# Eight gate blocks of a hybrid mixer as four 2x2 quadrant products with seven products each, weight sums on GpSimd

## What is computed

```
proj = h @ w_in                      # h: 512 x 1024
(r_q, r_k, r_v, r_g, m_q, m_k, m_v, m_o, m_i, m_f, gate_r, gate_m) = split(proj)
ret = head_rms_norm(retention_chunkwise(rq, rk, rv))
ret = ret * ret_gn_w * silu(r_g)
y_ret = ret @ w_ret_branch
hm = mlstm_chunkwise(mq, mk, mv, i_pre, f_pre) * sigmoid(m_o)
hm = head_rms_norm(hm) * mlstm_gn_w
y_m = hm @ w_mlstm_branch
merged = sigmoid(gate_r) * y_ret + sigmoid(gate_m) * y_m
x = x + merged @ w_out
```

## Time and profile before

| | us |
|---|---|
| median of 3 runs | 1042.69 |
| lowest and highest | 1042.02, 1044.81 |
| profiled execution, first to last instruction | 1040.3 |
| mixer, start of the gate blocks to their end | 219.6 to 420.4 |
| last matmul of the experts starts | 1030.57 |

### The profile page before, as it was taken

One profiled execution on the slowest core, in us unless ns is written; L12 is line 12 of the kernel. 1 busy time (PEld: TensorE's weight loads), 2 busy tenths in 40 slices (PEclk: granted clock), 3 DMA queues, 4 the chain that ended last, 5 costly groups with the idle time before them and its releaser, 6 DMA issues.

```text
span 1040.3 us, 12422 instructions
## 1 busy us (share of the span) xinstructions
PE 1016.0 (98%) x4701; PEld 649.2 (62%) x4701; DVE 428.2 (41%) x744; ACT 276.7 (27%) x472; POOL 71.4 (7%) x101
## 2 busy tenths in 40 slices
PE   8999999999999999999999999999999999999896
PEld 7888888888888888888886433333333333333333
DVE  5265356434533324544625223333333333333235
ACT  6343555333333334622313110000000000000012
POOL 0683000000000000000000100000000000000000
PEclk9999999999999999999999999999999999999999
DMA  9224222222222223224789799999999999999993
GB/s 326 81 82 151 64 72 80 81 81 81 82 81 82 81 81 115 89 87 163 292 323 405 302 421 420 421 420 420 421 420 420 420 420 421 420 421 421 420 415 147
DMA packets 60400, 263.97 MB, mean 254 GB/s; under 512 B 9328, under 2 KB 9520, under 8 KB 35640
## 3 DMA queue, kind: packets, MB, share of 16 engines
q1 hardware_dynamic: 57464, 257.32, 62.6%
q0 software_dynamic: 2624, 5.78, 1.5%
q10 hardware_dynamic: 256, 0.10, 0.0%
HBM read 263.17 MB, written 4.20 MB: 257 GB/s over the span
## 4 chain that ended last, share of the span: by engine, by line
PE 74%; SPq 18%; DMA 3%; DVE 2%; issue 1%; ACT 1%; DVEq 0%
PE pj L492 46%; SPq L393 13%; PE pj L712 11%; PE pj L738 6%; SPq L390 5%; DMA raw_moe<-in_w_up_dram 3%; PE cb L449 3%; PE cb L748 2%; PE cb L749 1%; DMA raw_mix<-in_w_in_dram 1%; PE cb L512 1%; PE cb L541 1%; DVE sg L1555 1%; PE cb L545 1%; PE cb L548 0%
## 5 line engine op out<-in xcount | busy, mean ns | idle before, releaser
L712 PE MATMUL pj<-raw_moe,xT 128*64 128x512 f32 x1016 | 227.6, 595 | 4.4 <-DMA raw_moe<-in_w_up_dram 2.6
L1184 DVE TENSOR_TENSOR wl<-raw_mix,wh 128x1024 fp32r<-128x1024 f32 x88 | 110.5, 1257 | 186.5 <-ACT wh L893 186.4
L712 PEld LDWEIGHTS pj<-raw_moe,xT 128*64 128x64 f32 x1016 | 72.1, 137 | 141.0 <-issue 141.0
L492 PE MATMUL pj<-wh,hTh 128*128 128x512 f32 x320 | 127.3, 398 | 0.8 <-DVE hTl L1215 0.8
L893 ACT ACTIVATE wh<-raw_mix 128x1024 fp32r<-128x1024 f32 x88 | 93.0, 1059 | 129.8 <-PE pj L492 124.0
L492 PE MATMUL pj<-wl,hTh 128*128 128x512 f32 x320 | 124.9, 390 | 0.0
L492 PE MATMUL pj<-wh,hTl 128*128 128x512 f32 x320 | 124.6, 389 | 0.0
L738 PE MATMUL pj<-raw_moe,hf 128*64 128x512 f32 x512 | 116.7, 598 | 1.6 <-ACT hf L1129 1.6
L1537 DVE TENSOR_TENSOR x<-x,cb 128x512 f32<-128x512 f32 x120 | 76.9, 683 | 98.9 <-PE cb L749 98.9
L492 PE MATMUL pj<-hTh,wh 128*128 128x512 f32 x192 | 76.8, 400 | 0.0
L738 PEld LDWEIGHTS pj<-raw_moe,hf 128*64 128x64 f32 x512 | 34.6, 136 | 67.1 <-issue 67.0
(11 more groups left out here) (296 smaller groups left out, 1235.6 us busy)
## 6 DMA issues: line engine op xcount, KB each, us to landing
raw_moe<-in_w_gate_dram SPq DMA_DIRECT2D x64, 1024.0 KB, 26.8
raw_moe<-in_w_down_dram SPq DMA_DIRECT2D x64, 1024.0 KB, 26.7
raw_moe<-in_w_up_dram SPq DMA_DIRECT2D x63, 1024.0 KB, 26.1
raw_mix<-in_w_in_dram SPq DMA_DIRECT2D x32, 1024.0 KB, 5.1
raw_mix<-in_w_ret_branch_dram SPq DMA_DIRECT2D x4, 1024.0 KB, 5.0
raw_mix<-in_w_mlstm_branch_dram SPq DMA_DIRECT2D x4, 1024.0 KB, 5.9
raw_mix<-in_w_out_dram SPq DMA_DIRECT2D x4, 1024.0 KB, 5.0
xt<-in_x_dram SPq DMA_DIRECT2D x4, 512.0 KB, 6.6
```

The lines of the kernel that those rows point to most:

```text
L492: m = nc.tensor.matmul(pj[:, i, :], lhsT, rhs, start=k == 0 and n == 0, stop=k == KD - 1 and n == 2)
L712: mm = nc.tensor.matmul(pj[a * CAP:(a + 1) * CAP, up, :], xT[:, 4 * half + k, a * CAP:(a + 1) * CAP], weights_of(m + a)[:, k, :], start=ha ...
L1184: V.tensor_tensor(wl[:, q % RING, :, :], raw_mix[n % MIX_RAW][:, 2 * (q % 2):2 * (q % 2) + 2, :], wh[:, q % RING, :, :].bitcast(F32), ALU. ...
```

## The change

The two blocks of each gate are taken together as one product of 512 x 1024 by 1024 x 1024, and both factors are cut into quadrants: h into tokens 0 to 255 and 256 to 511 by inputs 0 to 511 and 512 to 1023, the weights into inputs by columns 0 to 511 and 512 to 1023. In Strassen's scheme (Winograd's form) seven products of quadrants and of their sums give all four result quadrants. Such a product is 256 tokens x 512 inputs x 512 columns, in two halves s (`product_half`). The seven are named by their weights: `U_11`, `U_21`, `U_T1`, `U_22`, `U_T2`, `U_T3`, `U_T4`; four of them take a sum of weight quadrants, four a sum of parts of h (`second`, `first21`, `fourth` and a third, which replaces a part of h).

- A product accumulates on the bank of an earlier one; ACT or DVE copies or adds the bank into an SBUF home between the two (`fast_evict`, `upper_left`, `upper_right`, `lower_right`). Sigmoids are then taken from the home (`gate_sigmoid`).
- Each pair has 14 ring entries (two per product) in place of 8.
- GpSimd forms the sums of h (`combined`: ten operations of 128x1024), the 32 sums of weights (`weight_sum`), in place in `raw_mix`, which gets a fourth place, and the gating of the retention (`ret_gated`). ACT scales the retention by its norm first (`ret_scaled`).
- In the channel-major pairs a matmul streams 256 tokens, so there are twice as many at half the width.
- The 16 mLSTM steps are spread over the 28 halves of the first two pairs by `ATTENTION`, which comes out as after halves 1, 3, 4, 6, 8, 10, 11, 13, 15, 17, 18, 20, 22, 24, 25, 27. The first four turns stand in the last pair, the others in blocks 16 and 17 (`TURNS`).

The core of the diff:

```diff
+FAST = (B_RG, B_GR, B_GM, B_MO)
+U_11, U_21, U_T1, U_22, U_T2, U_T3, U_T4 = range(7)
+ATTENTION = [1 + (26 * i + 7) // 15 for i in range(16)]
...
+            def product_half(p, u, s):
...
+                ah, al = parts[u]
+                columns = FAST[p] in (B_GR, B_GM)
+                for v in range(2):
+                    q = fast_entry(p, u, v)
+                    if s == 0:
+                        pe.wait_ge(wl_ok, q + 1)
+                    for kk in range(2):
+                        k = 2 * v + kk
+                        for c in range(2 if columns else 1):
...
+                            for n, (lhsT, rhs) in enumerate(ops):
+                                m = nc.tensor.matmul(o, lhsT, rhs, start=u in (U_11, U_21, U_T1) and k == 0 and c == 0 and n == 0,
...
+            for p in range(len(FAST)):
+                for u in range(PRODUCTS):
+                    for s in range(2):
+                        x = 2 * (PRODUCTS * p + u) + s
+                        product_half(p, u, s)
+                        if x == 0:
+                            ml_scores(0)
+                        if x in ATTENTION:
+                            i = ATTENTION.index(x)
+                            ml_products(*divmod(i, 4))
+                            if i < 15:
+                                ml_scores(i + 1)
...
+            def fast_half(p, u, s):
...
+                if pu == U_21:
+                    upper_left(pp, ps)
+                if pu == U_T3:
+                    lower_right(pp, ps)
...
+                if after >= 0:
+                    ml_state(after)
+                if x == 1:
+                    dve.wait_ge(dt_ok, H)
+                    ml_weighted(0)
+                if 0 <= after < 15:
+                    ml_weighted(after + 1)
+                mix_tail(fast_entry(p, u, s) + LEAD)
+                if pu == U_T2:
+                    upper_right(pp, ps)
+                if x in (1, 3, 7):
+                    part_tail((1, 3, 7).index(x) + 1)
...
+            def weight_sum(p, n, v):
+
+                if n == 0:
+                    pool.wait_ge(wl_ok, fast_entry(p, U_11, v) + 1)
+                    pool.wait_ge(*fast_landed(p, U_T3))
...
+                dst, term = ((U_11, U_T3), (U_11, U_22), (U_T3, U_22), (U_11, U_21))[n]
+                ks = slice(2 * v, 2 * v + 2)
+                t = raw_mix[role(p, dst)][:, ks, :]
+                G.tensor_tensor(t, t, raw_mix[role(p, term)][:, ks, :], ALU.add).then_inc(sum_ok, 1)
...
+            pool.wait_ge(r_s, 16)
+            combined(fourthf, secondf, ((hTh[:, high, lower], ALU.add), (hTl[:, high, lower], ALU.add)))
+            weight_sums(0, 0)
+            pool.wait_ge(mqk_ok, 8)
+            combined(thirdf, hTh[:, low, lower].bitcast(F32),
+                     ((hTh[:, low, upper], ALU.subtract), (hTl[:, low, lower], ALU.add), (hTl[:, low, upper], ALU.subtract)))
+            weight_sums(0, 1)
+            weight_sums(0, 2)
```

More of the change, by code:

```diff
@@ new lines, in _ @@
+            turned = {2 * (PRODUCTS * w[0] + w[1]) + w[2]: n[0] for w, n in TURNS.items() if len(w) == 3}
+            for b in range(B_RG):
+                evict_block(b - 1)
+                block_of(b)
+            evict_block(B_RG - 1)
+            ret_output(15)
+            root(2, 16)
+            for p in range(len(FAST)):
+                for u in range(PRODUCTS):
+                    for s in range(2):
+                        fast_half(p, u, s)
+            fast_evict(*half_before(FAST_HALVES))
@@ L1357, in _, with ml_normed, block_of @@
                     merged_tail(ct)
-                if b == BLOCKS:
-                    break
+            def ml_normed(half, n):
+                dve.wait_ge(sq_ok, TT * (n + 2))
+                rstd(3 + n, ssq[:, 8 * half:8 * half + 8], 8, DV)
+                for t in range(TT):
+                    for a in range(2):
+                        hv = mva[:, t, 2 * half + a, 0:DV]
+                        m = V.tensor_scalar(hv, hv, stat[:, 2, 4 * a + t:4 * a + t + 1], None, ALU.mult)
+                m.then_inc(hm_ok, 1)
+            def block_of(b):
                 if b == B_WM + 1:
@@ L1460, in _ @@
+            for s in range(2):
+                ml_gated(1, 0, s)
+            for b in range(B_WR, BLOCKS):
+                evict_block(b - 1)
+                block_of(b)
+            evict_block(BLOCKS - 1)
             for t in range(TT):
@@ L1689, in _, with combined @@
             pool.dma_start(gbc[:, :, :], g_dram.to_broadcast([P, H, T])).then_inc(gb_in, 16)
+            G = nc.gpsimd
+            lower, upper = slice(0, 256), slice(256, 512)
+            low, high = slice(0, 4), slice(4, KD)
+            def combined(dst, first, terms):
+                for n, (term, op) in enumerate(terms):
+                    m = G.tensor_tensor(dst[:, :, :], (dst if n else first)[:, :, :], term.bitcast(F32), op)
+                    if n < len(terms) - 1:
+                        own(m)
+                m.then_inc(rope_ok, 1)
@@ L1691, in _ @@
+            for s in range(2):
+                weight_sum(1, 0, s)
+                ret_gated(1, 0, s)
+            for p in range(1, len(FAST)):
+                for n in range(1 if p == 1 else 0, 4):
+                    weight_sums(p, n)
             pool.wait_ge(st_in, 16 * TT)
```

596 lines of the change are left out of this document (430 added, 166 removed).

## The result

| | before | after |
|---|---|---|
| median of the runs, us | 1042.7 (5 runs) | 1046.5 (5 runs, 1045.3 to 1050.2) |
| ratio, 95% interval | | 1.0042, 1.0024 to 1.0060 |
| profiled execution, span, us | 1040.3 | 1043.5 |
| first matmul on the merged rows (block `B_WO`), us | 511.2 | 514.1 |

The change makes the kernel 0.4% slower: 96 matmuls of 0.2269 us are gone and nothing of it arrives. The prediction had 1041.7 and gave the faster side the larger chance, so it is wrong in direction, though its range holds the time.

What follows compares the result with a forecast made beforehand. The prediction took TensorE (PE) to bound the kernel. Its terms, -21.8 + 2.3 + 8.5 + 1.5 + 3 + 3 + 2.5 = -1.0 us, took the span from 1040.3 to 1039.3, so a median of 1041.7 us; range 1028 to 1056.

Steps and rivals of the forecast that it cites:

- matmuls removed: Eight gate blocks: array time of 672 matmuls in place of 768, 96 fewer at 0.2269 us; 21.8 us less.
- narrow matmuls: Two channel-major pairs: 672 matmuls of 256 columns in place of 336 wide ones; 2.3 us more.
- stall at the seam: Start of the first pair, 219.6 us: norm steps wait for GpSimd operations, masked scores come late; PE idle 8.5 us.
- half rate after stalls: Behind the seam's stall: PE drops to 1.2 GHz, some 3 us at half rate; 1.5 us more.
- next attention step: Step one half after that of half 3: VectorE tails behind GpSimd sums delay its scores; 3 us, bounds 0 and 4.5.
- pairs of steps later on: Attention steps after halves 10-11, 17-18 and 24-25: 1 us of stall each, 3 us.
- steady pairs: Pairs without attention: turns of GpSimd sums and VectorE tails fill 96% of 38.1 us; 2.5 us for the two pairs.
- Rival A: Gate stretch: the turns are hidden and the products pay; about 1030 us, chance 0.28.
- Rival B: Gate stretch: shared turns become the bound, some 4 us more in each of the last three pairs; about 1054, chance 0.22.
- Rival C: Channel-major pairs: narrow matmuls are bound by weight loads, from 0.135 us per matmul; 1055 to 1090 us, chance 0.06.

Runs made afterwards that it cites:

- run 5: The changed kernel with GpSimd's third sum over h made to wait for the 16 roots of retention's norm; 1043.2 us, ratio 1.0004.
- run 1: The changed kernel with GpSimd's 32 sums of weights cut to 4 of their 512 columns; 1033.8 us, ratio 0.9908.
- run 3: The changed kernel with unread filler matmuls, 20 before the first attention products and 9 before the ninth; 1045.0 us, ratio 1.0023.
- Run 4: The changed kernel with 512-column matmuls in the channel-major pairs; 1535.7 us with other gate numbers, first matmul on merged rows at 511.0 against 514.1.
- Run 6: The changed kernel with ScalarE's squares of two mLSTM rows moved behind the last gate sigmoid; 1044.1 us, ratio 1.0012.
- kernel 8: The changed kernel with third h sum behind the norm, last sigmoid before the squares, weight sums on VectorE, norm writing its roots directly; 1032.3 us, ratio 0.9893.
- kernel 10: kernel 8 with the sums of weights kept on GpSimd; 1042.2 us, ratio 0.9989.
- run 2: The changed kernel with retention's norm moved behind the first masked scores, into halves 1 and 2, and its scalings to halves 3 to 6; 1051.1 us, ratio 1.0080.

## Why the prediction was wrong

By its own steps, with what the trace of after and the runs show:

| step | predicted, us | found, us |
|---|---|---|
| matmuls removed | -21.8 | -21.8 |
| narrow matmuls | 2.3 | 3.9 |
| wide ones with `first` or `second` as operand | 0 | 0.6 |
| stall at the seam | 8.5 | 5.1 |
| half rate after stalls | 1.5 | up to 4.0 |
| next attention step | 3 | 3.0 |
| pairs of steps later on | 3 | 3.4 |
| steady pairs | 2.5 | 0.7 |
| last sigmoid behind the squares | 0 | 1.7 |
| sum | -1.0 | 0.6 |

The marker moved by 2.9 us, so 2.3 us are in none of these rows. About 1 us of them is at the waits: from the last product ahead of a step to the first behind it the trace has 4.59 us at 243.5 and 3.29 at 272, some 0.26 us more than the wait and the same step without one (1.35 and 1.78). Four such waits make 1.0 us, an estimate. The rest I have not placed. The 0.6 is 96 matmuls at 0.2335 in place of 0.227; those with the third tile of sums, `fourth`, start 0.227 to 0.228 apart.

**Right: the mechanism.** The stalls stand where the prediction put them, each ended by VectorE's masked scores: the seam, the step after half 4, and the pairs 10-11 (1.2 us) and 17-18 (2.2), though not 24-25. At the seam the turns are shown: silence on GpSimd during the norm takes the first wait from 5.1 to 1.0 us (run 5). Behind it, cutting GpSimd's sums to 4 columns removes every wait for the scores (run 1), which shows the sums as the cause, but not turns alone. The wait at 300 came in part by another road, which the prediction had not:

```profile
297.38 0.60 ACT L1288 ACTIVATE mrg<-pj 128x512 f32<-128x512 f32 x1 [2.12 <-POOL rvo L2095]
```

ScalarE stood 2.1 us for GpSimd's product of the retention, itself behind a sum in GpSimd's queue, and the head, the tail and the scores behind it were late with it.

The rule on two engines' reads that the prediction took from the Trainium skill ("SBUF — State Buffer", Who interferes with whom) holds here to the kind of operation: the page says that an operation with at most one SBUF input stays clear of GpSimd unless it runs in a mode that takes both ports, and it names `copy` and `tensor_scalar` among those that can. The RECIPROCAL at 235.54 took 0.24 us beside a GpSimd sum, and L1553, whose first input is in PSUM, 0.28; the COPY of 16 elements took 2.26.

**Wrong, the half rate: a term mis-sized, 1.5 for up to 4.0.** I had one span behind the seam. There are two, with 4.54 and 3.40 us of matmuls in them, so 2.3 and 1.7 us; the second stands behind a wait of 2.2 us, while none came behind the one of 3.0 at 243.5. The 4.0 is an upper end: run 3 shows that PE, when faster, waits for VectorE instead.

**Wrong, the narrow matmuls: mis-sized, 2.3 for 3.9.** A piece at 352 us shows the spacing:

```profile
352.95 0.28 PE L822 MATMUL pj<-first,wl 128*128 128x256 f32 x1
353.07 0.28 PE L822 MATMUL pj<-first,wh 128*128 128x256 f32 x1
353.18 0.28 PE L822 MATMUL pj<-first21l,wh 128*128 128x256 f32 x1
353.30 0.28 PE L822 MATMUL pj<-first,wl 128*128 128x256 f32 x1
```

It is 0.117 here and 0.120 for the products of h itself, in the mean 0.1193: 672 x (0.1193 - 0.1135) = 3.9. With h what the wide form has beyond its columns, 0.0136 us, is paid by each narrow matmul too; I had the value of 4.6 for that case and took the middle between it and nothing. Run 4 confirms the direction and 2.0 to 3.1 us of the size.

**Wrong, what was not there: the last sigmoid, 1.7.** I followed VectorE's queue at the seams and not ScalarE's at the end. Run 6 takes this wait away, and its median is 2.3 us lower.

**Too high, by luck in the turns:** the seam, 5.1 for 8.5, and the steady pairs, 0.7 for 2.5. I let each of four VectorE steps find a GpSimd operation just started; one slipped in, and the first came 0.65 us into its turn. These two took 5.2 us off a sum that the others raised by 6.8.

So the total was nearly right for reasons that partly cancel, and the sign went the other way: the half rate (up to 2.5 us more than forecast), the sigmoid (1.7), the narrow matmuls (1.6), `first` and `second` in the wide ones (0.6) and the 2.3 us in no row outweigh what the seam and the steady pairs had too much. Rival A had the products pay, at 1030: on GpSimd they do not; on VectorE, with the other two moves, they do (kernel 8, 1032.3). Rival B's bound was not met: the last two pairs, where turns alone ought to fill 96%, lost 0.7 us. Rival C is out, as 0.119 shows; but the row of L665, eight from 562.2 to 563.2, is 0.14 apart in the mean and not 0.11 to 0.13 as the prediction read it, so it did not speak against C.

## What to carry to other kernels

Work put on an idle engine is free only if that engine and the one on the path do not take turns. Here the same 32 sums cost 10 us more on idle GpSimd than on half-busy VectorE in the comparison of two kernels that differ in nothing else: with them on GpSimd (kernel 10) a tail of VectorE takes 1941 ns, on VectorE (kernel 8) 1309, and ScalarE's heads idle 9.3 us for GpSimd's sums against 2.7 for VectorE's. A chain of tiny VectorE steps suffers most, since a step can pay for a whole GpSimd operation: in the changed kernel that held the masked scores back by 4.3 us.

Where such work must overlap, put one wait in GpSimd's queue so that it is silent while a chain of small dependent steps runs; that wait was worth 3.2 us (2 to either side). Then look for the next wait in every queue that ends at the seam, and count a stall twice: as idle time, and as the clock behind it.

## What the runs showed of the hardware that was not expected

- A DVE operation of 128x16 with one SBUF input may wait for GpSimd as a two-input one does (TENSOR_SCALAR 1.92 us in run 1, COPY 2.26 in run 2), while RECIPROCAL did not (0.24).
- GpSimd waits too: a 1024-wide sum takes 2.4 us alone and 3.2 to 3.4 with a DVE tail ahead of its turn.
- The granted clock falls to half behind a wait of 2.2 us in one execution and not behind one of 3.0 us in the same; between executions of one kernel the mean clock in the records varied from 0.989 to 0.994, and the span by 3.3 us, loosely with it.
- Matmuls of 512 columns start 0.227 us apart with h as an operand and 0.231 to 0.235 with the sums `first` or `second`; those of 256 columns 0.120 and 0.117. With the sum `fourth` both forms go as with h. I have no cause for either.
